# The channel mixer's products by Strassen's scheme over pairs of frame tiles

## What is computed

```python
for l in range(DEPTH):                      # 2
    h = rmsnorm(x, norm1_g[l])
    proj = h @ w_in[l]                      # 1024 x 8208: q, k, v, r, fz, B, C, x_in, g_A, g_B
    # A: gated linear attention by chunks of 64 frames, 4 heads, with a state; norm; silu(r); w_oa
    # B: B * conv3(C * x_in), then w_ob
    x = x + (sigmoid(g_A) * y_A + sigmoid(g_B) * y_B) @ w_o[l]
    h2 = rmsnorm(x, norm2_g[l])
    hid = silu(h2 @ w_ffn_gate[l]) * (h2 @ w_ffn_up[l])     # 1024 x 2816 each
    x = x + hid @ w_ffn_down[l]                             # 2816 x 1024
return rmsnorm(x, final_g)
```

## Time and profile before

| what | value |
|---|---|
| median of three runs | 4570.1 us |
| lowest, highest run | 4569.0, 4690.22 us |
| profiled execution, core 1: span | 4567.5 us |
| profiled execution, core 0, the longest span of its die | 4572.4 us |
| profiled execution, core 7, the longest span of all | 5327.9 us |
| core 1: PE, PEld, DVE, ACT, POOL busy | 4523.2, 2057.2, 2014.1, 1551.3, 190.7 us |
| core 1: DMA moved | 870.25 MB |

### The profile page before, as it was taken

The page is one execution under the profiler, slowest core; times in us unless marked ns, Lnnn a source line. Parts: engine busy times, 40 slices in busy tenths (PEclk is TensorE's granted clock), DMA queues, the critical chain, the costliest instruction groups (busy, mean ns, idle before and its releaser), DMA issues.

```text
span 5327.9 us, 63749 instructions; the slowest of 8 cores (4567.5 to 5327.9 us)
## 1 busy us (share of the span) xinstructions
PE 5292.3 (99%) x21996; PEld 2239.1 (42%) x21996; DVE 2023.3 (38%) x3171; ACT 1561.7 (29%) x2996; POOL 187.5 (4%) x348
## 2 busy tenths in 40 slices
PE   9999999999999999999999999999999999999998
PEld 4444444444444444444444444444444444444443
DVE  4555555544522222222244444444444322222222
ACT  4344533342311111111235235234234112222111
POOL 1000000000000000000000000000000000000000
PEclk9999999888888888888888888888888888888887
DMA  9977775466574645555444544544434544444442
GB/s 196 237 219 197 206 209 176 135 176 175 141 216 157 172 161 161 170 165 169 144 142 139 173 143 141 168 136 146 162 135 140 180 157 153 145 161 147 150 157 75
DMA packets 124489, 870.25 MB, mean 163 GB/s; under 512 B 14512, under 2 KB 14640, under 8 KB 48048
## 3 DMA queue, kind: packets, MB, share of 16 engines
q1 hardware_dynamic: 115776, 770.75, 41.8%
q0 software_dynamic: 7392, 92.80, 12.3%
q10 hardware_dynamic: 1008, 2.62, 0.2%
HBM read 868.48 MB, written 148.37 MB: 191 GB/s over the span
## 4 chain that ended last, share of the span: by engine, by line
PE 95%; DMA 4%; ACT 0%; issue 0%; DVE 0%; ACTq 0%; POOL 0%; POOLq 0%; SPq 0%; DVEq 0%
PE pb L329 89%; PE pb L341 5%; DMA sb_wsl<-w_mix 2%; DMA sc_mix_cv<-sb_wsl 1%; PE pb L635 1%; DMA sc_mix_k<-sb_wsl 0%; DMA sb_xT<-x 0%; DMA sc_mix_o<-sb_wsl 0%; DMA sc_mix_ob<-sb_wsl 0%; PE pb L520 0%; DMA sb_wsl<-sc_mix_k 0%; ACT sb_arena L499 0%; ACT sb_arena L502 0%; DVE sb_xT L809 0%; ACT L499 0%
## 5 line engine op out<-in xcount | busy, mean ns | idle before, releaser
L329 PE MATMUL pb<-sb_hT,sb_wsl 128*128 128x512 bf16 x8728 | 2239.9, 424 | 5.3 <-DMA sb_wsl<-w_mix 4.7
L329 PEld LDWEIGHTS pb<-sb_hT,sb_wsl 128*128 128x128 bf16 x8728 | 915.6, 106 | 1292.0 <-issue 1075.7
L329 PE MATMUL pb<-sb_arena,sb_wsl 128*128 128x512 bf16 x3324 | 854.9, 425 | 0.2 <-DMA sb_wsl<-w_mix 0.2
L329 PE MATMUL pb<-sb_hT,sb_arena 128*128 128x512 bf16 x3136 | 829.7, 436 | 0.0
L775 DVE TENSOR_TENSOR sb_arena<-pb,sb_tmp 128x512 bf16<-128x512 f32 x352 | 243.5, 692 | 1049.6 <-PE pb L329 1045.1
L770 ACT ACTIVATE sb_tmp<-pb 128x512 f32<-128x512 f32 x352 | 210.2, 597 | 1432.0 <-PE pb L329 1386.6
L329 PEld LDWEIGHTS pb<-sb_arena,sb_wsl 128*128 128x128 bf16 x3324 | 354.5, 107 | 489.9 <-issue 414.6
L329 PEld LDWEIGHTS pb<-sb_hT,sb_arena 128*128 128x128 bf16 x3136 | 341.1, 109 | 486.4 <-issue 486.4
L329 PE MATMUL pb<-sb_wsl,sb_hT 128*128 128x512 bf16 x2048 | 524.1, 419 | 10.1 <-DMA sb_wsl<-w_mix 5.1
L461 DVE TENSOR_TENSOR sb_xT<-pb,sb_xT 128x512 f32<-128x512 f32 x256 | 172.1, 689 | 777.4 <-PE pb L329 685.4
L329 PE MATMUL pb<-sb_arena 128*128 128x512 bf16 (+1 forms) x2052 | 463.0, 401 | 0.0
(11 more groups left out here) (97 smaller groups left out, 2896.4 us busy)
## 6 DMA issues: line engine op xcount, KB each, us to landing
sb_wsl<-sc_mix_cv SPq DMA_DIRECT2D x116, 1280.0 KB, 6.0
sb_arena<-sc_ffn_f SPq DMA_DIRECT2D x98, 1024.0 KB, 4.9
sb_wsl<-sc_ffn_f SPq DMA_DIRECT2D x78, 1024.0 KB, 5.0
sb_arena<-sc_ffn_d SPq DMA_DIRECT2D x70, 704.0 KB, 4.4
xs<-sb_xT SPq DMA_DIRECT2D x48, 1024.0 KB, 4.8
sb_xT<-xs SPq DMA_DIRECT2D x96, 512.0 KB, 9.4
sb_wsl<-sc_ffn_d SPq DMA_DIRECT2D x58, 704.0 KB, 4.5
sb_wsl<-sc_mix_ob SPq DMA_DIRECT2D x30, 1024.0 KB, 4.9
```

Source lines behind the costliest of these rows:

```text
L329: return lambda pe: pe.matmul(out, lhsT, rhs, start=first, stop=last)
```

## The change

The channel mixer works on a pair of tiles (1024 frames) with one level of Strassen's scheme in Winograd's form: each product of 2 x 2 blocks takes seven block products, M1 to M7, instead of eight. The rows of a block are 128 x 128 weight chunks in the output direction, halves of the 1024 input channels (gate and up) or chunks 2c and 2c + 1 of hid (down), and the two tiles of frames.

- **Weights' sums.** For each layer 66 pieces of f32 weights (128 x 1024) are loaded, seven bf16 blocks are made from them by GpSimd (two copied, five summed), and stored to HBM. This is spread over the mixer steps of the layer (in layer 0 from the third on) and replaces the casts by DMA. Mixer weights of layer 1 are cast in halves of 64 partitions during layer 0's channel mixers.
- **Activation sums.** `norm_h2` makes h2 during the next mixer step and stores it as bf16; `load_h2` brings two tiles back, `sums_h2` makes five sums of them on VectorE. `sums_ho` makes seven right-hand sides from the four blocks of hid of one chunk pair.
- **Products.** For each of 22 gate or up blocks: M3 and M4 into banks W and V, then M5 on top of W, M2 on top of V, M1 into Z (on top of V + M3), M7 on top of Y = Z - c12 and M6 on top of Z - c21. ScalarE keeps the intermediate values s3, c12, c21 in SBUF, VectorE writes Z and Y in PSUM. M7 and M6 of a block are issued after M3 and M4 of the next ("late"). The down projection does the same with products of 11 matmuls. So a pair of tiles has 22 x 7 x 4 + 4 x 7 x 11 = 924 matmuls; two tiles had 2 x 528 = 1056.
- **Slots and tiles.** Weight slots are four of 5120 columns in a mixer, five of 3584 in a channel mixer, over the same memory. Several tiles move into a larger arena.
- **The end.** Squares are taken as x becomes final, in layer 1; the last pair is scaled and stored at the end, 16 chunks. A Ln of one column comes ahead of it, so that its table is loaded.

```diff
-            for p_ in range(11):
-                sl, wk, w = get_block("f%d" % p_)
-                for j in range(2):
-                    fc = p_ * 2 + j
...
-            for dc in range(8):
-                sl, wk, w = get_block("d%d" % dc)
-                b = bank()
-                fm_group(b, w, wk, 0, hid, lambda fc: [("hid", fc)], nk=NFC)
-                residual(s, b, dc)
-                done_block(sl)
...
+    bl = [("%s%d" % (n, p), 1, 28 * 128, None) for p in range(NPAIR) for n in ("g", "u")]
+    return bl + [("d%d%s" % (n, m), 1, NPAIR * 128, None) for n in range(4) for m in PROD]
+
+
+
+PROD = ["M3", "M4", "M5", "M2", "M1", "M7", "M6"]
+WSUM = {"M7": 0, "M6": 1, "M2": 2, "M1": 3, "M5": 4, "M4": 5, "M3": 6}
...
+        def prep_jobs(l):
+            A12, A21, A22, A11 = (pin[:, j, :] for j in range(4))
+            def pace():
+                tk.wait(tk.E["pool"], tk.E["pe"].sem, tk.E["pe"].cnt)
+            def total(nm, x, o, y):
+                m = WSUM[nm]
+                op("pool", ["pin"], [("pout", m)], lambda h: h.tensor_tensor(out=pout[:, m, :], in0=x, in1=y, op=o))
+            def first():
+                pace()
+                op("pool", ["pin"], [("pout", 5), ("pout", 6)],
+                   lambda h: h.tensor_copy(out=pout[:, 5:7, :], in_=pin[:, 2:4, :]))
+                total("M1", A11, ALU.add, A22)
+            def second():
+                pace()
+                total("M2", A21, ALU.add, A22)
+                total("M5", A11, ALU.add, A12)
+            def third(i):
+                pace()
+                total("M6", A21, ALU.subtract, A11)
+                total("M7", A12, ALU.subtract, A22)
+                if i + 1 < NPIECE:
+                    prep_load(l, i + 1)
+                ...
+                dma("pool", R1("pout", 7), [("prep", l, i)], posem, lambda q: q.dma_start(out=dst, in_=pout))
+
+            yield lambda: prep_load(l, 0)
+            for i in range(NPIECE):
+                yield first
+                yield second
+                yield lambda i=i: third(i)
+                for _ in range(5):
+                    yield lambda: None
...
+        def sum_y(hf, to=None, key="rstd"):
+            assert dc_of[hf] == KC
+            dc_of[hf] = 0
+            b = bank()
+            mms([BK(b)], [(mm(pb[b][:, :], ones32[:, :], sq[hf][:, 0, :], True, True), ["ones32", ("sq", hf)])])
+            rstd_of(b, to, key)
+
+        def out_y(hf, t, kc, r, key, wide=4):
+
+            op("dve", [("xT", hf, kc), key, "pk"], [("xT", hf, kc)],
+               lambda h: h.scalar_tensor_tensor(out=xT[hf][:, kc, :], in0=xT[hf][:, kc, :], scalar=pkc(100 + kc),
+                                                in1=r, op0=ALU.mult, op1=ALU.mult))
...
+        def norm_h2(l, t, dst, keys, rest=4, gap=0):
+
+            yield from norm_h(t % 2, gain2(l), dst, keys, rest, gap)
+            dma("sp", keys, [("h2", l, t)], h2sem[1][t % 2],
+                lambda q: q.dma_start(out=h2_d[l][t].rearrange("p (a b) -> p a b", a=KC), in_=dst))
+
...
+            def add(bo, b, sk, s_, alu):
+                op("dve", [sk], [BK(bo)] if bo == b else [BK(bo), BK(b)],
+                   lambda h: h.tensor_tensor(out=pb[bo][:, :], in0=pb[b][:, :], in1=s_, op=alu))
+            def keep(b, k, t_, func=AF.Copy):
+                op("act", [], [BK(b), k], lambda h: h.activation(out=t_, in_=pb[b][:, :], func=func))
+            def gate(i, b):
+                keep(b, ("gt", i), gt[i], AF.Silu)
+            def swiglu(pr, i, b):
+                out, k = ((bt[pr % 2][:, i, :], ("bt", pr % 2, i)) if i < 2 else (ho[pr][:, 3 - i, :], ("ho", pr, 3 - i)))
+                op("dve", [("gt", i)], [BK(b), k], lambda h: h.tensor_tensor(out=out, in0=pb[b][:, :], in1=gt[i], op=ALU.mult))
+            def sums_ho(c):
+                S, X = ho[c], bt[c % 2]
+                xk = [("bt", c % 2, i) for i in range(2)]
+                hk = lambda *at: [("ho", c, i) for i in at]
+                op("dve", xk + hk(0, 1), hk(3, 4), lambda h: h.tensor_tensor(out=S[:, 3:5, :], in0=X, in1=S[:, 0:2, :], op=ALU.subtract))
+                op("dve", hk(0, 1), hk(2), lambda h: h.tensor_tensor(out=S[:, 2, :], in0=S[:, 1, :], in1=S[:, 0, :], op=ALU.add))
+                op("dve", xk + hk(0, 1), hk(5, 6), lambda h: h.tensor_tensor(out=S[:, 5:7, :], in0=X, in1=S[:, 1::-1, :], op=ALU.add))
+            def onto_x(b, hf, dc):
+                op("dve", [], [BK(b), ("xT", hf, dc)],
+                   lambda h: h.tensor_tensor(out=xT[hf][:, dc, :], in0=xT[hf][:, dc, :], in1=pb[b][:, :], op=ALU.add))
+                if l == DEPTH - 1:
+                    squares.append((hf, dc))
...
+                W, V, Z, Y = (bank() for _ in range(4))
+                out = (lambda i, b, pr=pr: swiglu(pr, i, b)) if up else gate
+                four("M3", W, False)
+                keep(W, "s3", s3)
+                yield
+                four("M4", V, False)
+                add(Z, V, "s3", s3, ALU.add)
+                yield
+                yield from some_late()
+                some_squares(2)
+                four("M5", W, True)
+                keep(W, "c12", c12)
+                out(0, W)
+                yield
+                four("M2", V, True)
+                keep(V, "c21", c21)
+                out(1, V)
+                yield
+                four("M1", Z, True)
+                add(Y, Z, "c12", c12, ALU.subtract)
+                add(Z, Z, "c21", c21, ALU.subtract)
+                yield
+                def last7(four=four, out=out, Y=Y):
+                    four("M7", Y, True)
+                    out(2, Y)
+                def last6(four=four, out=out, Z=Z, sl=sl):
+                    four("M6", Z, True)
+                    out(3, Z)
+                    done_block(sl)
+                late.extend([last7, last6])
+                if up:
+                    late.append(lambda pr=pr: sums_ho(pr))
...
+                if n == 0:
+                    e_ = NPAIR - 1
+                    part("M3", W, False, 0, 8)
+                    yield from some_late()
+                    read_to_end[0] = s
+                    part("M3", W, False, 8, e_)
+                    part("M4", V, False, 0, 5)
+                    yield
+                    part("M3", W, False, e_, NPAIR)
+                    keep(W, "s3", s3)
+                    part("M4", V, False, 5, NPAIR)
+                    add(Z, V, "s3", s3, ALU.add)
+                    yield
+                else:
+                    part("M3", W, False)
+                    keep(W, "s3", s3)
+                    yield
+                    part("M4", V, False)
+                    add(Z, V, "s3", s3, ALU.add)
+                    yield
+                    yield from some_late()
+                some_squares(2)
+                part("M5", W, True)
+                keep(W, "c12", c12)
+                yield
+                part("M2", V, True)
+                keep(V, "c21", c21)
+                some_squares(2)
+                yield
+                part("M1", Z, True)
+                add(Y, Z, "c12", c12, ALU.subtract)
+                add(Z, Z, "c21", c21, ALU.subtract)
+                onto_x(W, 1, 2 * n)
+                onto_x(V, 0, 2 * n + 1)
+                yield
+                def last7(part=part, Y=Y, n=n):
+                    part("M7", Y, True)
+                    onto_x(Y, 0, 2 * n)
+                def last6(part=part, Z=Z, n=n):
+                    part("M6", Z, True)
+                    onto_x(Z, 1, 2 * n + 1)
+                    if n % 2 and l < DEPTH - 1:
+                        for hf in range(2):
+                            store_x(hf, 2 * j + hf, n // 2, xs_d, "xs")
+                late.extend([last7, last6])
...
+        spread(list(prep_jobs(0)), 2, F0)
+        spread([lambda bi=bi, hf=hf: cast_piece(1, bi, hf) for bi in range(len(BLOCKS["mix"])) for hf in range(2)], F0, M1)
+        spread(list(prep_jobs(1)), M1, M1 + NT)
...
+        def sides(s):
+            p, t = steps[s]
+            k, l = PH[p]
+            hk = lambda i: [("hT", i, kc) for kc in range(KC)]
+            n = (t + 1) % 2
+            if k == "mix":
+                yield from lead(3)
+                if t:
+                    yield from norm_h2(l, t - 1, hT[n], hk(n))
+                yield from lead(2)
+                if t < NT - 1:
+                    yield from do(load_x, n, t + 1, p == 0)
+                    yield from lead(16)
+                    yield from norm_h(n, l * 8, hT[n], hk(n))
+                    if t == 0 and l:
+                        yield from slowly(0, 0, 2)
+                else:
+                    yield from do(load_h2, l, 0)
+                    yield from until_read(s)
+                    yield from do(load_h2, l, 1)
+                    yield from lead(6)
+                    yield from sums_h2()
+            else:
+                yield from lead(16)
+                if t == 0:
+                    yield from slowly(0, 0, 7)
```

(27 more changed lines are left out.)

500 lines of the change are left out of this document (306 added, 194 removed).

## The result

The changed kernel is faster: its time is 0.9621 of the kernel before, interval [0.9599, 0.9642], from runs of 4392.87, 4393.32 and 4402.87 us against 4569.0 and 4570.1. The prediction, 4378 us, is 0.958, and its range held these runs. (In three of the six runs of the changed kernel and four of the six of the kernel before, a die ran at a lower granted clock; so the medians over all six, 4774.5 against 4761.6, compare nothing, and 4774.5 lies far above the forecast's range, which has no term for it.) The profiled execution took 4402.87 us. The gain is real and nearly the size forecast; what needs explaining is some 25 us in the slowest core, and a loss of clock on other chips that the forecast left out.

A forecast was written before the change was run, and what follows sets the result against it. TensorE (PE) bounds all four stages, so time is matmuls times spacing: 4567.5 - 222 = 4345.5, plus 4 + 6 + 7 + 4 + 9 = 4375.5, with 2.6 about 4378 us. Range 4340 to 4455 us.

The forecast's parts named there:

- main term: Channel mixers: 924 matmuls instead of 1056 per pair of tiles, 200.3 us a pair; eight pairs save 222 us.
- unknown operations: Product groups: VectorE's PSUM-writing operation, 0 to 26 us, and three bf16 additions, 0 to 50 us; both taken as 0.
- the end of 50 us: Gate groups: if the three bf16 additions run at f32's rate, M7 is 0.57 us late, 88 times.
- Norms: Layer 1's final norms: ScalarE's table loads, Ln and Exp delay its copies, 6 us, ends 0 and 20.
- moved norm: Channel mixer's norm, begun three groups into the next mixer: 0 to 2 us in 14 steps, taken as 7 us.
- First down group: M3's last matmul waits for the last three sums: 0.2 to 0.8 us, 8 times, taken as 4 us.
- Tail: After the last residual: sixteen scalings and 4.2 MB to store, 6 to 12 us longer, taken as 9.
- the one on transfers: Weight loads, thinnest in the down phase: 0 to 16 us, taken as 4, since landings of 5.0 are under 9.5 us.
- rival on late weights: Down phase: landings of 12 us against 9.5 of lookahead cost 156 us, half if only layer 0; chance 0.09.
- GpSimd: Mixers: weight sums delay the attention's small operations on GpSimd's queue, but some 6.8 us are free; taken as nothing.
- slower rival: Mixers: GpSimd waits for a piece's load and blocks the attention; at 22 us each, 4900 us; chance 0.04.

## Why the prediction came out as it did

**The main term was right.** In layer 1's channel mixers 4 x 200.3, seven norms of 1.1, 2 for the first down groups and 6 for the final norms make 817 us; it took 821.0 on every full-clock core. The spacing is 0.2157 us (28 matmuls from 3549.33 to 3555.37 us in core 5, the forecast had 0.2154), and an eighth product put the time back to that of before.

**The unknown operations were costed right.** The subtraction that writes PSUM took 695 ns against 691 for the row I took it from the earlier trace rows. The three bf16 additions took 0.693 + 0.420 + 0.685 = 1.80 us where f32's rate gives 3.1, so the end of 50 us wasn't met. (The Trainium skill, "VectorE: DVE Perf Modes", section "Mode 2×_1P — pack two bf16 into one 32-bit read", has two results per cycle for such operands; the estimate worked out from it was 1.8 us, and the trace agrees.) The doubled additions show how thin that was: the margin ended after about 1.2 us.

**Norms: 6 us forecast, 14 measured, and none for the moved one.** The waits on L959 are 14.2 us in 15, also in layer 0, where a norm for the last tile runs in a pair. One of them, core 5, layer 1 (start us, us):

```profile
3781.11 1.28 ACT L519 ACT_TABLE_LOAD   x1
3782.40 0.69 ACT L519 ACTIVATE sb_rstd<-pb,sb_epsb 128x512 f32<-128x512 f32 x1
3783.18 0.63 ACT L520 ACTIVATE sb_rstd<-sb_rstd 128x512 f32<-128x512 f32 x1
3783.72 0.58 ACT L962 ACTIVATE sb_arena<-pb 128x512 f32<-128x512 f32 x1
...
3784.37 1.28 ACT L962 ACT_TABLE_LOAD   x1
3784.58 0.69 DVE L959 TENSOR_TENSOR pb<-pb,sb_wring 128x512 f32<-128x512 f32 x1
3785.38 0.70 DVE L959 TENSOR_TENSOR pb<-pb,sb_arena 128x512 f32<-128x512 f32 x1
...
3785.42 0.81 PE L950 MATMUL pb<-sb_arena,sb_wring 128*128 128x512 bf16 x3 [1.51 <-DVE pb L959]
```

Table load, Ln and Exp take 2.6 us in one piece ahead of the copy in L962, the two VectorE operations follow it, and PE starts 1.51 us late. The place is as forecast, the piece is shorter: the second table load comes behind the copy, not ahead of it. What I left out are the norm of the last tile in each layer and the last group of each phase, whose late products have nothing left to run beside. The moved norm, 7 us forecast, cost nothing: the wait behind the gate chain was 11.1 us in 16 before and is 9.9 to 10.7 in 15 now. First down group: 2.5 us in 8, forecast 4. Tail: 20.5 to 21.5 against 13.1, 7.4 to 8.4 longer, forecast 9.

**The step that failed is the one on transfers.** I took 4 us, on the argument that a landing of 5.0 us is well under 9.5 us of lookahead, and named the down phase as the thin place. Measured over the 808 us of the stage without casts: 13 us on core 5, 30 on core 3. Two things were wrong. A median landing says nothing of the worst stretch: the DMA share over the stage was 0.84 (forecast 0.76) and 1.00 during the longest wait, where x stood ahead in SP's queue. And in seven of the eight cores most of the waiting was for blocks of 896 KB in the up and gate groups (12.3 us in core 3, against 8.9 for sc_dn), not for those of the down phase. Spacing x took both down, a slot less raised both. I also left out that PE runs at half clock behind a longer wait, 8.5 us on top of 21.2 in core 3. And I built the sum on one core, where the slowest counts: this term alone puts 17 us between core 3 and core 5. The rival on late weights had this mechanism at 156 us, or 78 if in layer 0 alone, more than twice what core 3 lost.

That the sum met core 5 to half a microsecond is luck. There the norms and the transfers cost 27 us where I took 10; the moved norm, the first down groups and the tail cost 10 where I took 20; the other 7 us come from the start and the mixers, which were shorter than I took them. The time forecast for the kernel, with 2.6 added, was 15 to 25 us too low.

**GpSimd: nothing forecast, 1 to 7 us measured.** PE's wait for the attention's late operands (L759) is 5.9 us in four in core 3, 7.0 in core 1 and 0.6 in core 5; before it was 1.5 in one. Behind it VectorE waited 30.6 us for GpSimd's small operation in core 3. Small, but the edge of a cliff, as the doubled sums show. The slower rival was right about the queue and wrong about what it waits for: the store of its own result. VectorE does pay for GpSimd's company: the scaling with two inputs from SBUF of 750 ns in the kernel before (its L677) takes 802 now (L810), and 860 with GpSimd's sums doubled. The norm's scaling (L559) takes 836 in the mixers, and 745 in the channel mixers, where GpSimd makes no sums. (The Trainium skill, "GPSIMD Engine Reference", section "8. Key points", says that GpSimd shares its SBUF interfaces with VectorE operations of two SBUF inputs; the trace agrees, with 7 and 15% for the scaling.) PE in layer 1's mixers doesn't feel it: 1330.2 us against 1325.7, and the reductions of seven norms, 1.1 us each, have moved there.

**What no step had.** I had no term for the granted clock of a die. On the two chips of the experiments a die ran the changed kernel with its clock at 0.81 for stretches of 4 to 15 us, 40 to 60 us of the gain in the runs compared, where the kernel before lost little or nothing in its own (a mean granted clock of 0.991 at the lowest). They lie mostly in the channel mixers, where PE now has VectorE, ScalarE and the DMA engines busy beside it. With eight products, where the other engines do less beside each matmul, the weaker die had 9 to 12 such stretches, with more waits (the additions doubled) 7 to 13, against 17 to 21 in the changed kernel: that fits a part of the density, but it is one profile each. And on the chip of the result it was the other way round: cores 0 to 3 had nine or ten stretches of 4 to 8 us at 0.81 under the kernel before, 46 to 49 us or 9 us of its time, and no core had one under the changed kernel in its profile. Why a die does it, and why only one of two, stays open.

## What to carry to other kernels

When PE bounds every stage, fewer matmuls pay at their spacing, but the other engines then have a smaller period: lay out one period by latencies, and double the new work on an engine in an experiment to see how much of the margin is left. Judge transfers by the fullest stretch and the order in their queue, not by a median landing, and remember that a wait of some microseconds also lowered the clock behind it. Move loads that nobody waits for soon apart from those that PE needs next, and build the sum for the slowest core.

## What the runs showed of the hardware

A VectorE subtraction that reads and writes PSUM (128x512, f32) takes 695 ns, no more than one that reads PSUM and writes SBUF. A bf16 addition of 1024 elements, all in SBUF, takes 690 ns where f32 took 1217. A GpSimd addition of 128x256 f32 into bf16 takes 846 ns in core 3 and 856 in core 5, and 857 there if each is made twice. Behind a wait of 3.8 us the granted clock was 0.51 for 6 us. The VectorE scaling of 128x512 with two inputs from SBUF takes 750 ns where GpSimd is busy for 4% of the span, 802 and 860 where it is for 22 and 33%. And the granted clock of one die was 0.81 for 15 us at a time, 21 times in a run of the changed kernel, on a chip where the kernel before had a mean of 0.991 to 0.998; on another chip the kernel before had such stretches, of 4 to 8 us, and the changed kernel none.
